# Gate and up products of a SwiGLU feed-forward network by seven block products in place of eight

## The chip, the cores and the metric

One core of a Trainium2 chip runs the kernel. TensorE (PE) multiplies, VectorE (DVE), ScalarE (ACT) and GpSimd (POOL) do the elementwise work, SyncE (SP) issues the loads of weights. The metric is the device time of one execution in microseconds (us).

## The reference, cut to what matters

One decoder layer works on 1056 token rows of width 1024: 1024 of a prompt and 32 samples. A mixer (a matrix memory beside sparse attention) ends in an output projection, a residual sum and a layer normalisation. The feed-forward network (FFN) follows, with 2816 hidden columns:

```python
D_FF = -(-8 * D_MODEL // (3 * 256)) * 256        # 2816
ALPHA = (2 * DEPTH) ** 0.25
h = jax.nn.silu(x @ w_gate) * (x @ w_up)          # 1056 x 2816
y = layer_norm(ALPHA * x + h @ w_down, g2, b2)
```

Everything is float32. The change concerns `x @ w_gate` and `x @ w_up` alone.

## The kernel before, in words

A float32 operand is kept as two parts: a high part (rounded to the type that TensorE takes) and a low part (the rest). `PARTS` lists the three products high-high, high-low and low-high that stand for one product. ScalarE makes high parts by a copy, GpSimd (for `x` of the mixer also VectorE) makes low parts by a subtraction.

**First normalisation.** `x` comes out of the output projection in nine row tiles (eight of 128, one of 32 that holds the samples), each in two column halves. VectorE adds the product bank to the residual (L1673, ALPHA x plus the product), takes statistics, adds epsilon, ScalarE takes the root (`std`), VectorE inverts it and centres the row (L1696). TensorE transposes the tile, ScalarE puts it with gain and bias into `y_acc` (`put_turned`), VectorE makes the high part `xs` (`high_of`), GpSimd the low part (L1725) and scales `y_acc` by ALPHA (L1731), so that `y_acc` can take the down product's sums.

**FFN.** The hidden columns are taken in 11 groups of 256 (`GROUPS`), each as two units `u` of 128. A unit needs 128 columns of the gate and of the up weights; SP loads the two pieces, 512 KB each, into one raw buffer `graw` (`sp_ffn.gate`), ScalarE copies the 2048 columns to the high part (`high`, L1865), GpSimd makes the low part (`low`, L1947). Two such pairs of split weights stand in turns. TensorE takes the 1056 rows in three chunks of 352 columns; per chunk, gate and up are each a sum over eight k tiles of three products: 2 x 2 x 3 x 8 x 3 = 288 matmuls of 352 columns per group (L1830), and 3168 in all. ScalarE takes silu of the gate bank (L1873), VectorE multiplies it by the up bank (L1911), copies the high part (`tensor_copy`, L1915) and subtracts to the low part (L1919).

The down product of group g-1 stands between the two units of group g: 144 matmuls of 352 columns (L1808), whose 24 banks VectorE adds to `y_acc` (L1816). The loops run over the groups on every engine; the last two groups' down products are done in the second normalisation (`pe_y`), ahead of the output.

The order on each engine is the order of the code; semaphores hold an instruction back. On SP the load of a unit waits for the low part of the one before (`g_lo`), since there is one raw buffer. GpSimd's order in the loop is `low(g, 1)`, `low(g + 1, 0)`, `low_down(g)`; VectorE's is the hidden columns of unit 0, the adds of the down product, the hidden columns of unit 1.

## Time and profile before

| what | value |
|---|---|
| three runs | 1586.88, 1587.2 and 1593.45 us; median 1587.2 |
| span of the profiled execution | 1586.6 us (no separate time is given for it) |
| TensorE busy | 1546.0 us, 97% |
| VectorE, ScalarE, GpSimd busy | 49%, 28%, 26% |
| gate and up matmuls (L1830) | 3168, 32% of the span in the chain that ended last |
| down matmuls in the loop (L1808) | 1296, 13% |

The span is the time from the first to the last recorded instruction. The chain that ended last follows the work back from the end, at each step to what released it. In a timeline row, the bracket behind an instruction is the idle time ahead of it on its engine and the instruction that ended it. Matmuls overlap in the pipeline, so a matmul's duration in a row is longer than the pitch at which they follow each other; a pitch is the time of a whole chain step divided by its matmuls.

### The profile page before, as it was taken

Reading aid. Unit: us, or ns where it says so; the run is one execution under the profiler, and the core shown is the slowest. Engines: PE = TensorE matmul, PEld = TensorE weight load, DVE = VectorE, ACT = ScalarE, POOL = GpSimd, SP = SyncE. Lnnn points to the kernel's source line nnn. Section 1 sums busy time; section 2 is a strip of 40 time slices with the busy share of each in tenths; the row PEclk is TensorE's granted clock in tenths of the full one; section 3 lists DMA queues with packets and bytes.
Section 4 is the critical chain, followed back from the end, with each engine's and each line's share of the span. In section 5 each row is a group of like instructions: output and inputs, shape, how many; then the busy total and the mean of one; then the engine's idle time right before and its main releaser. Section 6 shows DMA issues by size and latency. Waiting matters only on the chain.

```text
span 1586.6 us, 26851 instructions
## 1 busy us (share of the span) xinstructions
PE 1546.0 (97%) x10593; PEld 1435.2 (90%) x10593; DVE 772.3 (49%) x1664; ACT 451.5 (28%) x929; POOL 412.3 (26%) x405
## 2 busy tenths in 40 slices
PE   7999999999999998899999999999999999999998
PEld 7986799999996666687899999999999999999986
DVE  2008599999965664563653323324132332313146
ACT  4336423222145564361352120221112012111100
POOL 3620256321110002453683221221122122112200
PEclk9999999999999999999999999999999999999999
DMA  5210231222317004543202101101111111111011
GB/s 187 72 44 19 65 101 41 71 83 85 104 46 258 28 27 130 161 128 123 67 27 80 53 27 54 54 30 51 54 54 27 54 54 36 45 54 54 1 61 76
DMA packets 117236, 110.52 MB, mean 70 GB/s; under 512 B 16218, under 2 KB 102366, under 8 KB 117122
## 3 DMA queue, kind: packets, MB, share of 16 engines
q1 hardware_dynamic: 116482, 106.80, 21.6%
q0 software_dynamic: 640, 2.10, 0.4%
q8 instruction: 84, 1.38, 0.3%
q14 instruction: 30, 0.25, 0.0%
HBM read 88.82 MB, written 19.95 MB: 69 GB/s over the span
## 4 chain that ended last, share of the span: by engine, by line
PE 58%; POOL 0%; DVE 0%; issue 0%; DVEq 0%
PE bank L1830 32%; PE bank L1808 13%; PE bank L1599 6%; PE bank L1993 3%; PE bank L1988 0%; PE bank L1748 0%; PE bank L1167 0%; PE bank L1595 0%; PE bank L1170 0%; POOL c_and_n_sample L1317 0%; PE bank L1133 0%; PE bank L1153 0%; PE bank L1182 0%; PE bank L1103 0%; POOL mv_by_sample L1313 0%
## 5 line engine op out<-in xcount | busy, mean ns | idle before, releaser
L1830 PE MATMUL bank<-x_split,gate_up_split 128*128 128x352 f32 x3168 | 509.9, 322 | 0.0
L1830 PEld LDWEIGHTS bank<-x_split,gate_up_split 128*128 128x128 f32 x3168 | 507.3, 188 | 0.1
L2284 PE MATMUL bank<-w_split,xT_split 128*128 128x256 f32 (+1 forms) x1950 | 247.7, 284 | 3.7 <-POOL w_split L2517 2.0
L2284 PEld LDWEIGHTS bank<-w_split,xT_split 128*128 128x128 f32 (+1 forms) x1950 | 234.3, 187 | 8.2 <-issue 3.7
L1911 DVE TENSOR_TENSOR hidden<-silu,bank 128x352 f32<-128x352 f32 x66 | 34.4, 521 | 408.5 <-ACT silu L1873 408.5
L1808 PE MATMUL bank<-hidden_split,weight_split 128*128 128x352 f32 x1296 | 209.2, 322 | 0.0
L1808 PEld LDWEIGHTS bank<-hidden_split,weight_split 128*128 128x128 f32 x1296 | 208.0, 188 | 0.0
L1947 POOL TENSOR_TENSOR gate_up_split<-gate_up,gate_up_split 128x2048 fp32r<-128x2048 f32 x22 | 104.1, 4734 | 370.7 <-ACT gate_up_split L1865 370.7
L2622 DVE TENSOR_SCALAR_CACHE_REDUCE chosen<-scores,level 128x384 uint8<-128x384 f32 (+2 forms) x198 | 174.3, 943 | 1.2
L1816 DVE TENSOR_TENSOR y_acc<-y_acc,bank 128x352 f32<-128x352 f32 x216 | 112.5, 521 | 84.6 <-PE bank L1808 83.4
L2341 PE MATMUL bank<-xT_split,w_split 128*128 128x352 f32 x864 | 138.4, 322 | 0.0
L2341 PEld LDWEIGHTS bank<-xT_split,w_split 128*128 128x128 f32 x864 | 138.2, 188 | 0.0
L1873 ACT ACTIVATE silu<-bank 128x352 f32<-128x352 f32 x66 | 30.6, 464 | 364.3 <-PE bank L1830 364.2
L2517 POOL TENSOR_TENSOR w_split<-w_unit,w_split 128x2048 fp32r<-128x2048 f32 (+1 forms) x16 | 72.2, 4514 | 147.7 <-ACT w_split L2362 147.7
L1951 POOL TENSOR_TENSOR weight_split<-down_weight,weight_split 128x2048 fp32r<-128x2048 f32 x10 | 46.1, 4606 | 159.5 <-ACT weight_split L1879 159.5
L1599 PE MATMUL bank<-out_weight_split,x_split 128*128 128x512 f32 (+1 forms) x342 | 81.6, 396 | 0.0
L1599 PEld LDWEIGHTS bank<-out_weight_split,x_split 128*128 128x128 f32 (+1 forms) x342 | 63.4, 186 | 15.5
L2410 ACT ACTIVATE stage<-bank 128x256 f32<-128x256 f32 x80 | 30.7, 384 | 161.2 <-PE bank L2284 150.7
L1879 ACT ACTIVATE weight_split<-down_weight 128x2048 fp32r<-128x2048 f32 x10 | 19.1, 1915 | 186.6 <-PE bank L1808 186.6
L545 ACT ACTIVATE attention_weights<-attention_weights,row_minima 128x1024 f32<-128x1024 f32 (+7 forms) x64 | 49.1, 768 | 46.9 <-DVE row_minima L476 46.8
L476 DVE CUSTOM_DVE_ANT_0 attention_weights<-bank,scores 128x512 f32<-128x512 f32 (+1 forms) x48 | 30.1, 666 | 50.2 <-PE bank L387 50.2
L1865 ACT ACTIVATE gate_up_split<-gate_up 128x2048 fp32r<-128x2048 f32 x22 | 42.1, 1913 | 22.5 <-DMA gate_up<-in_w_up_dram 22.4
(310 smaller groups left out, 1703.3 us busy)
## 6 DMA issues: line engine op xcount, KB each, us to landing
w_unit<-in_w_in_dram SPq DMA_DIRECT2D x15, 1024.0 KB, 5.7
gate_up<-in_w_gate_dram SPq DMA_DIRECT2D x22, 512.0 KB, 4.0
gate_up<-in_w_up_dram SPq DMA_DIRECT2D x22, 512.0 KB, 5.2
down_weight<-in_w_down_dram SPq DMA_DIRECT2D x11, 1024.0 KB, 4.9
scratch_dram<-feature_stage SPq DMA_DIRECT2D x36, 176.0 KB, 1.8
scores<-in_x_prompt_dram SPq DMA_DIRECT2D x8, 512.0 KB, 3.9
out_dram<-stage SPq DMA_DIRECT2D x32, 128.0 KB, 1.7
out_weight<-in_w_out_dram SPq DMA_DIRECT2D x16, 256.0 KB, 6.2
```

Source lines behind the costliest of these rows:

```text
L545: act.activation(x, x, ACT.Exp, bias=lows[:, n % 4, e, chunks[n] - 1:chunks[n]], scale=-1.0, accum_out=rowsum[:, o % 2, 2 * p + e:2 * p + ...
L1599: mm = pe.matmul(product_bank(m)[0:rows(i), :], mix(i, a)[:, k, :], wo[h][:, k, b, :], start=(k == 0 and (a, b) == PARTS[0]), stop=(i < LA ...
L1808: mm = pe.matmul(PS[6 + n % 2][:, 0:cols.stop - cols.start], wds[:, a, k, d * P:(d + 1) * P], hs[:, 2 * s + k, b, cols], start=(k == 0 and ...
L1816: dve.tensor_tensor(y, y, PS[6 + n % 2][:, 0:cols.stop - cols.start], ALU.add).then_inc(d_added, 1)
L1830: mm = pe.matmul(PS[2 * c + w][:, 0:CH], gs[u][:, a, w, k, :], xs[:, b, k, c * CH:(c + 1) * CH], start=(k == 0 and (a, b) == PARTS[0]), st ...
L1947: pool.tensor_tensor(gs[u][:, 1], graw, gs[u][:, 0].bitcast(F32), ALU.subtract).then_inc(g_lo, 1)
L1951: pool.tensor_tensor(w[:, 1], wdraw, w[:, 0].bitcast(F32), ALU.subtract).then_inc(wd_lo, 1)
L1993: mm = pe.matmul(bank, hs[:, 2 * s + k, a, tile_cols(i)], w[:, b, k, 512 * half:512 * half + 512], start=False, stop=(s == 0 and k == 1 an ...
L2284: mm = pe.matmul(out, tokens, w[:, b, k, :], start=((k, a, b) == terms[0]), stop=((k, a, b) == terms[-1]))
L2341: mm = pe.matmul(bank[:, 0:CH], wsplit[n_unit % 2][:, a, k, (m % 2) * P:(m % 2 + 1) * P], xs1[:, b, k, c * CH:(c + 1) * CH], start=(k == 0 ...
L2517: pool.tensor_tensor(lo, wraw[n >= 4][:, k], hi.bitcast(F32), ALU.subtract).then_inc(w_lo, 1)
L2622: dve.tensor_scalar(chosen[i], score[i], level_f[:, n:n + 1], 0.0, op, ALU.add, accum_out=count[:, n:n + 1]).then_inc(topk_step, 1)
```

## The change

The 1056 rows of `x` and the 1024 inner columns are halved, and so are the 256 columns of a group. A matrix (the gate or up weights of one group; 22 in all) then has four blocks A11, A21, A12, A22 of 512 x 128, and its product is formed from seven block products (`multiply`, j = 0 to 6) in place of eight, after Strassen and Winograd. Each block product is two chunks of 272 and 256 columns, four k tiles and `PARTS`: 24 matmuls (L2049), 168 per matrix, 3696 in all. The order of a matrix's factors is A11, A12, three weight sums with A12 changed among them, A22 (`part_source`), against `XPARTS`. Banks 0 and 1, 2 and 3, 4 and 5 each gather two or three block products; banks 6 and 7 stay with the down product.

- **Weights.** SP loads a matrix's two halves of 512 KB into one raw buffer (`load`, L1972); half 1 of the next matrix waits for the low part of j = 6 of this one. A ring of four slots holds the split blocks; ScalarE copies 128x512 to the high part (`high_part`, L1962), GpSimd subtracts to the low part (`low_part`, L1966). GpSimd forms four weight sums per matrix (`weight_sums` and `last_weight_sum`, L2174 to L2184) ahead of the low part of j = 2, in place in the raw buffer. The down weights pass through the same ring as four parts.
- **Sums of x.** T1 to T4 are formed by VectorE in the first normalisation (`halves_of`), split by ScalarE and GpSimd. The row tiles come in the order 0, 1, 2, 3, samples, 4, 5, 6, 7.
- **Results.** ScalarE puts the first product into SBUF (`put_p1`, L2104). VectorE adds bank 2 and 3 to it twice (`products_16`, L2190, and `products_165`, L2196) and makes the second to fourth quarter of the result from it and a bank (`result`, L2215: r1, r2, r3). For an up matrix it also multiplies by silu (`hide`, L2229) and splits (`split_hidden`, L2237 and L2241). TensorE's next writes to a bank wait for the result that reads it: j = 0 of the next matrix waits for r2, j = 3 for r3.
- The scaling by ALPHA moves into the first down product's add. The reloads of ScalarE's function tables fall from the loop.

The core of the diff (what stands beside it is the order of the tiles and the stores of samples):

```diff
+HT = T // 2
+CO, CW = (0, 272), (272, HT - 272)
+raw = put("gate_up", R0, KD * 2 * P).rearrange("p (k n) -> p k n", k=KD)
+A11, A21, A12, A22 = raw[:, 0:4, 0:P], raw[:, 0:4, P:2 * P], raw[:, 4:8, 0:P], raw[:, 4:8, P:2 * P]
+RING_W = 4
...
+stages = []
+for g in range(GROUPS):
+    stages += [("gate", g)] + ([("down", g - 1)] if 0 < g < GROUPS - 1 else []) + [("up", g)]
+parts = [(kind, g, j) for kind, g in stages for j in range(4 if kind == "down" else 7)]
...
+XPARTS = (B11, B21, T2, T3, T1, B22, T4)
+BANK_OF = (0, 0, 2, 4, 2, 0, 4)
+BEGINS = (0, 2, 3, 5)
...
+def part_free(eng, e):
...
+def part_source(e):
+    kind, g, j = parts[e]
+    if kind == "down":
+        return slots_raw[:, e % RING_W, 1, :].rearrange("p (k n) -> p k n", k=2)
+    return (A11, A12, A11, A21, s1_sum, A12, A22)[j]
...
+def high_part(act, e):
+    kind, g, j = parts[e]
+    n = stage_no_of(kind, g)
+    part_free(act, e)
+    if kind == "down":
+        act.wait_ge(wd_in[j % 2], 16 * (2 * g + j // 2 + 1))
+    elif j in (0, 1, 6):
+        act.wait_ge(raw_in[j > 0], 16 * (n + 1))
+    else:
+        act.wait_ge(summed, summed_no(n, j))
+    act.activation(slot(e, 0), part_source(e), ACT.Copy).then_inc(slot_hi, 1)
+def low_part(pool, e):
+    pool.wait_ge(slot_hi, e + 1)
+    pool.tensor_tensor(slot(e, 1), part_source(e), slot(e, 0).bitcast(F32), ALU.subtract).then_inc(slot_lo, 1)
...
+    def load(n, half):
+        kind, g = ("gate", "up")[n % 2], n // 2
+        if n == 0:
+            sp.wait_ge(norms["first"]["nT"], 2 * 5)
+        elif half == 0:
+            before = part_no[("gate", "up")[(n - 1) % 2], (n - 1) // 2, 0]
+            sp.wait_ge(summed, summed_no(n - 1, 5))
+            sp.wait_ge(slot_lo, before + 4)
+        else:
+            before = part_no[("gate", "up")[(n - 1) % 2], (n - 1) // 2, 0]
+            sp.wait_ge(slot_lo, before + 7)
+        k = slice(4 * half, 4 * half + 4)
+        sp.dma_start(raw[:, k, :], weights[n % 2][:, k, 2 * P * g:2 * P * g + 2 * P]).then_inc(raw_in[half], 16)
...
+    def multiply(n, j, c):
+        e = part_no[("gate", "up")[n % 2], n // 2, j]
+        pe.wait_ge(slot_lo, e + 1)
+        if n == 0:
+            if j < 2:
+                pe.wait_ge(x1_lo, (6, 10)[c])
+            elif j < 6:
+                pe.wait_ge(x1_lo, (lows_before(6), lows_before(8))[c] + j - 1)
+            else:
+                pe.wait_ge(x1_lo, lows_before(TILES) + c + 1)
+            if j in (2, 3):
+                pe.wait_ge(added, 2 * TILES)
+        elif j in (0, 2, 3):
+            pe.wait_ge(combined, combined_no(n - 1, {0: "r2", 2: "p165", 3: "r3"}[j], c))
+        if j == 1:
+            pe.wait_ge(p1_put, 2 * n + c + 1)
+        if j == 4:
+            pe.wait_ge(combined, combined_no(n, "p16", c))
+        if j == 5:
+            if n % 2:
+                pe.wait_ge(h_made, 16 * (n // 2) + c + 1)
+            else:
+                pe.wait_ge(silu_done, silu_no(n // 2, 0, c))
+        if j == 6:
+            pe.wait_ge(combined, combined_no(n, "r1", c))
+        for k in range(4):
+            for a, b in PARTS:
+                mm = pe.matmul(PS[BANK_OF[j] + c][:, 0:CW[c]], slot(e, a)[:, k, :],
+                               XPARTS[j][:, b, k, CO[c]:CO[c] + CW[c]],
+                               start=(j in BEGINS and k == 0 and (a, b) == PARTS[0]),
+                               stop=(k == 3 and (a, b) == PARTS[-1]), skip_group_check=True)
+        mm.then_inc(product, 1)
...
+def weight_sums(eng, n):
+    e = part_no[("gate", "up")[n % 2], n // 2, 0]
+    for half in range(2):
+        eng.wait_ge(raw_in[half], 16 * (n + 1))
+    if n:
+        eng.wait_ge(slot_lo, part_no[("gate", "up")[(n - 1) % 2], (n - 1) // 2, 4] + 1)
+    s1 = s1_sum if n else s1_first
+    eng.tensor_tensor(s1, A21, A22, ALU.add).then_inc(summed, 1)
+    eng.tensor_tensor(A21, A11, A21, ALU.subtract).then_inc(summed, 1)
+    eng.wait_ge(slot_lo, e + 1)
+    eng.wait_ge(summed, summed_no(n, 3))
+    eng.tensor_tensor(A11, s1, A11, ALU.subtract).then_inc(summed, 1)
+def last_weight_sum(eng, n):
+    e = part_no[("gate", "up")[n % 2], n // 2, 0]
+    eng.wait_ge(slot_lo, e + 2)
+    eng.wait_ge(summed, summed_no(n, 2))
+    eng.tensor_tensor(A12, A12, A11, ALU.subtract).then_inc(summed, 1)
...
+def products_16(dve, n, c):
+    dve.wait_ge(product, product_no(n, 2, c))
+    dve.wait_ge(p1_put, 2 * n + c + 1)
+    dve.tensor_tensor(p16[:, c, 0:CW[c]], p1[:, c, 0:CW[c]], PS[2 + c][:, 0:CW[c]], ALU.add).then_inc(combined, 1)
+def products_165(dve, n, c):
+    dve.wait_ge(product, product_no(n, 4, c))
+    dve.wait_ge(combined, combined_no(n, "p16", c))
+    dve.tensor_tensor(p1[:, c, 0:CW[c]], p1[:, c, 0:CW[c]], PS[2 + c][:, 0:CW[c]], ALU.add).then_inc(combined, 1)
...
+    def matrix(kind, g):
+        n, e = stage_no_of(kind, g), part_no[kind, g, 0]
+        more(e)
+        put_p1(act, n, 0)
+        put_p1(act, n, 1)
+        for j in range(1, 7):
+            more(e + j)
+            if kind == "gate" and j != 2 and j != 3:
+                q = {1: 0, 4: 1, 5: 2, 6: 3}[j]
+                silu(act, g, q, 0)
+                silu(act, g, q, 1)
+            if n == 2 * GROUPS - 1 and j in (4, 6):
+                last_high((j - 4) // 2)
...
+    def matrix(kind, g):
+        n = stage_no_of(kind, g)
+        up = kind == "up"
+        if up:
+            hide(g, 0, 0)
+            hide(g, 0, 1)
+        products_16(dve, n, 0)
+        products_16(dve, n, 1)
+        if up:
+            split_hidden(g, 0)
+        for c in range(2):
+            products_165(dve, n, c)
+            result(dve, n, 1, c)
+        if up:
+            hide(g, 1, 0)
+            hide(g, 1, 1)
+            split_hidden(g, 1)
+        result(dve, n, 2, 0)
+        result(dve, n, 2, 1)
+        if up:
+            hide(g, 2, 0)
+            hide(g, 2, 1)
+            split_hidden(g, 2)
+        result(dve, n, 3, 0)
+        result(dve, n, 3, 1)
+        if up:
+            hide(g, 3, 0)
+            hide(g, 3, 1)
+            split_hidden(g, 3)
...
+    def halves_of(t):
+        i = SWEEP2[t]
+        c1, c = first_half(i), second_half(i)
+        dve.wait_ge(nm["nput"], 2 * t + 1)
+        if i < 4 or i == LAST:
+            dve.tensor_copy(B11[:, 0, :, c1], yh[:, 0:4, 0, c1]).then_inc(x1_hi, 1)
+        if i >= 4:
+            dve.tensor_tensor(T1_raw[:, :, c], yh[:, 0:4, 1, c], yh[:, 0:4, 0, c], ALU.subtract).then_inc(t_sum, 1)
+        dve.wait_ge(nm["nput"], 2 * t + 2)
+        if i < 4 or i == LAST:
+            dve.tensor_copy(B21[:, 0, :, c1], yh[:, 4:8, 0, c1]).then_inc(x1_hi, 1)
+        if i >= 4:
+            done = 4 * SUMMED.index(i)
+            dve.tensor_tensor(T3_raw[:, :, c], yh[:, 4:8, 1, c], yh[:, 0:4, 1, c], ALU.subtract).then_inc(t_sum, 1)
+            dve.wait_ge(t_sum, done + 1)
+            dve.tensor_tensor(T2_raw[:, :, c], yh[:, 4:8, 1, c], T1_raw[:, :, c], ALU.subtract).then_inc(t_sum, 1)
+            dve.tensor_copy(B22[:, 0, :, c], yh[:, 4:8, 1, c]).then_inc(x1_hi, 1)
+            dve.wait_ge(t_sum, done + 3)
+            dve.tensor_tensor(T4_raw[:, :, c], yh[:, 4:8, 0, c], T2_raw[:, :, c], ALU.subtract).then_inc(t_sum, 1)
...
+    for t in range(TILES - 3):
+        lows(t)
+    low_part(pool, 0)
+    low_part(pool, 1)
+    lows(TILES - 3)
+    low_part(pool, 2)
+    low_part(pool, 3)
+    low_part(pool, 4)
+    lows(TILES - 2)
+    low_part(pool, 5)
+    lows(TILES - 1)
```

The order of the instructions moves at three places. On GpSimd, in the loop over groups, the program before ran (`gate_up_split` are the two pairs of split weights, ISA rows are its semaphore operations):

```order
L1947 TENSOR_TENSOR gate_up_split_138<-gate_up,gate_up_split_138 128x2048
L1946 ISA
L1947 TENSOR_TENSOR gate_up_split_137<-gate_up,gate_up_split_137 128x2048
L1951 TENSOR_TENSOR weight_split<-down_weight,weight_split 128x2048
L1956 REGISTER_ALU
L1956 COMPARE_AND_BRANCH
```

and the changed one, from one matrix's first weight sum to the split of the down weights:

```order
L2174 TENSOR_TENSOR weight_sum<-gate_up 128x512
L2175 TENSOR_TENSOR gate_up<-gate_up 128x4x128
L2178 TENSOR_TENSOR gate_up<-weight_sum,gate_up 128x4x128
L2184 TENSOR_TENSOR gate_up<-gate_up 128x4x128
L1966 TENSOR_TENSOR weight_split<-gate_up,weight_split 128x512 x2
L1966 TENSOR_TENSOR weight_split<-weight_sum,weight_split 128x512
L1966 TENSOR_TENSOR weight_split<-gate_up,weight_split 128x512 x2
L1966 TENSOR_TENSOR weight_split<-down_weight,weight_split 128x512 x4
```

Two subtractions of 2048 columns per group have become 14 of 512 columns and eight sums; the four sums stand one behind the other, ahead of the third low part of their matrix.

On VectorE, from the fifth block product of an up matrix on (`product` is p1, `hidden_sum` the result's quarter, `bank` is in PSUM, the rest in SBUF):

```order
L2196 TENSOR_TENSOR product_154<-product_154,bank 128x272
L2215 TENSOR_TENSOR hidden_sum<-product_154,bank 128x272
L2196 TENSOR_TENSOR product_154<-product_154,bank 128x256
L2215 TENSOR_TENSOR hidden_sum<-product_154,bank 128x256
L2229 TENSOR_TENSOR hidden<-hidden,hidden_sum 128x272
L2229 TENSOR_TENSOR hidden<-hidden,hidden_sum 128x256
L2237 CAST hidden_split<-hidden 128x272
L2237 CAST hidden_split<-hidden 128x256
L2241 TENSOR_TENSOR hidden_split<-hidden,hidden_split 128x272
L2241 TENSOR_TENSOR hidden_split<-hidden,hidden_split 128x256
L2215 TENSOR_TENSOR hidden_sum<-product_154,bank 128x272
L2215 TENSOR_TENSOR hidden_sum<-product_154,bank 128x256
```

Ahead of the two L2215 rows that end it (r2, for which TensorE's next matrix waits) stand six instructions on operands in SBUF (two products, two copies, two subtractions); before, the three instructions of a chunk's hidden columns read its bank at once, and nothing of the next chunk stood behind them in the same bank.

On GpSimd, at the start of the first gate matrix (L1830 and L1833 are low parts of T2, T3, T1 and B22 of a row tile, L1966 are weights):

```order
L1966 TENSOR_TENSOR weight_split<-gate_up,weight_split 128x512 x2
L1830 TENSOR_TENSOR x_sums<-x_sums_raw,x_sums 128x4x128 x2
L1830 TENSOR_TENSOR x_split<-x_split_raw,x_split 128x4x128
L1833 TENSOR_TENSOR x_split<-y_acc,x_split 128x4x128
L1966 TENSOR_TENSOR weight_split<-gate_up,weight_split 128x512 x2
L1966 TENSOR_TENSOR weight_split<-weight_sum,weight_split 128x512
L1830 TENSOR_TENSOR x_sums<-x_sums_raw,x_sums 128x4x128 x2
L1830 TENSOR_TENSOR x_split<-x_split_raw,x_split 128x4x128
L1833 TENSOR_TENSOR x_split<-y_acc,x_split 128x4x128
L1966 TENSOR_TENSOR weight_split<-gate_up,weight_split 128x512
```

The low parts of the first weights stand between those of `x`: parts 2 to 4 behind the low parts of row tile 6's quarter, part 5 behind the next tile's.

## Rows read from the trace of the kernel before

**Rows 1.** The page, part 1: busy us (share of the span) xinstructions.
```profile
PE 1546.0 (97%) x10593; PEld 1435.2 (90%) x10593; DVE 772.3 (49%) x1664; ACT 451.5 (28%) x929; POOL 412.3 (26%) x405
```

**Rows 2.** The chain that ended last, in time: start us, us, engine, output, line.
```profile
793.88 5.59 PE bank L1599 x24
...
876.34 23.09 PE bank L1808 x144
899.43 46.10 PE bank L1830 x288
...
1452.87 69.16 PE bank L1830 x432
```

**Rows 3.** TensorE timeline, two stretches: start us, us, line, shapes, count.
```profile
187.26 8.40 PE L2284 MATMUL bank<-w_split,xT_split 128*128 128x256 f32 x69 [1.18 <-POOL w_split L2517]
...
320.13 22.89 PE L2284 MATMUL bank<-w_split,xT_split 128*128 128x256 f32 x192
342.85 0.28 PE L2284 MATMUL bank<-w_split,sample_x_split 128*64 128x256 f32 x1
```

**Rows 4.** Groups by line and form: busy us, mean ns of one; VectorE within 870 to 1450 us.
```profile
L1725 POOL TENSOR_TENSOR x_split<-y_acc,x_split 128x512 fp32r<-128x512 f32 x16 | 20.8, 1302 | 11.5 <-DVE x_split L1702 11.5
...
L2410 ACT ACTIVATE stage<-bank 128x256 f32<-128x256 f32 x80 | 30.7, 384 | 161.2 <-PE bank L2284 150.7 <-PE bank L2301 5.5 <-PE bank L2266 4.8
L1638 ACT ACTIVATE out_weight_split<-out_weight 128x512 fp32r<-128x512 f32 x16 | 8.8, 632 | 19.4 <-DMA out_weight<-in_w_out_dram 19.4
...
L1919 DVE TENSOR_TENSOR hidden_split<-hidden,hidden_split 128x352 fp32r<-128x352 f32 x50 | 26.2, 524 | 1.4
L1915 DVE CAST hidden_split<-hidden 128x352 fp32r<-128x352 f32 x50 | 17.1, 343 | 1.4
```

**Rows 5.** DMA issues: transfer, queue, count, KB each, median us to landing.
```profile
gate_up<-in_w_gate_dram SPq DMA_DIRECT2D x22, 512.0 KB, 4.0
gate_up<-in_w_up_dram SPq DMA_DIRECT2D x22, 512.0 KB, 5.2
```

**Rows 6.** VectorE and GpSimd timelines, single instructions near 707 and 1086 us.
```profile
705.43 0.69 DVE L1631 TENSOR_TENSOR x_split<-mixT,x_split 128x512 fp32r<-128x512 f32 x1 [0.24 <-ACT x_split L1621]
...
708.35 1.78 DVE L1631 TENSOR_TENSOR x_split<-mixT,x_split 128x512 fp32r<-128x512 f32 x1
...
707.84 1.74 POOL L1631 TENSOR_TENSOR x_split<-mixT,x_split 128x512 fp32r<-128x512 f32 x1
...
1086.35 4.94 POOL L1947 TENSOR_TENSOR gate_up_split<-gate_up,gate_up_split 128x2048 fp32r<-128x2048 f32 x1 [17.10 <-ACT gate_up_split L1865]
...
1086.80 0.52 DVE L1816 TENSOR_TENSOR y_acc<-y_acc,bank 128x352 f32<-128x352 f32 x1
```

**Rows 7.** TensorE and ScalarE timelines near 1045 us: start us, us, idle before, what ended it.
```profile
1037.62 12.55 PE L1830 MATMUL bank<-x_split,gate_up_split 128*128 128x352 f32 x77
...
1045.64 0.46 ACT L1873 ACTIVATE silu<-bank 128x352 f32<-128x352 f32 x1 [5.91 <-PE bank L1830]
```

**Rows 8.** VectorE timeline of the first normalisation, row tile 6.
```profile
793.11 0.69 DVE L1673 SCALAR_TENSOR_TENSOR x_tm<-x_tm,bank 128x512 f32<-128x512 f32 x1 [1.45 <-PE bank L1599]
...
797.22 0.91 DVE L1696 TENSOR_SCALAR x_tm<-x_tm,moments,rstd 128x1024 f32<-128x1024 f32 x1
```

**Rows 9.** TensorE timeline: three pauses, the idle time before in brackets.
```profile
612.58 1.20 PE L714 MATMUL bank<-sample_scores,square 32*128 32x288 f32 x4 [1.40 <-DVE mixT L519]
...
650.15 0.27 PE L1080 MATMUL bank<-mixT,mkT 128*32 128x32 f32 x8 [2.25 <-DVE mq_scaled L1342]
...
668.67 0.50 PE L1066 MATMUL bank<-g_split,head_rows_split 128*128 128x512 f32 x1 [1.94 <-DVE kT L1335]
```

**Rows 10.** Stretches around them: us, TensorE busy (x), granted clock, DMA share, GB/s.
```profile
613.00:618.00 5.00, 5.00 (x28) 0.66 0.72 209
650.00:656.00 6.00, 5.85 (x113) 0.72 0.74 295
666.00:672.00 6.00, 4.06 (x34) 1.00 0.18 59
```

## The forecast

> **What bounds the kernel now.** I read the page first: TensorE is busy 97% of the span, the next engine 49% [rows 1]. The page's busy share is not yet the limit, so I read the chain of waits next. From 876 us on it has TensorE steps alone: 144 down matmuls, 288 gate and up matmuls, and so on to 1522 us, where the last run of 432 (the second unit of group 9 and both of group 10) ends [rows 2]. In this stretch nothing but matmuls counts: what leaves TensorE there leaves the span, and every wait put onto TensorE is added to it. The other engines have slack on average, but a share of busy time says nothing of the order in which they work; so the question is whether the new chain TensorE, VectorE, GpSimd, ScalarE keeps TensorE fed at each handover.
>
> **What leaves TensorE.** 288 matmuls of 352 columns take 46.10 us [rows 2], a pitch of 160.1 ns; a matrix is half of this, 23.05 us. For 256 columns, 192 matmuls took 342.85 - 320.13 = 22.72 us, 118.3 ns each [rows 3]. No 272 occurs; the straight line through both points gives 0.435 ns a column and 125.3 ns. A block product is 12 x 125.3 + 12 x 118.3 ns = 2.92 us, a matrix of seven 20.46 us. Over 22 matrices that takes off 22 x (23.05 - 20.46) = **56.9 us**. Bounds: at a cost in proportion to columns (116.4 and 123.7 ns) it is 63.4; at the slowest dense stretch of 256, 8.76 us for 72 or 121.7 ns [rows 3], and 7 ns more for 272, it is 44.4. I take the line, since both its points are long runs without a break.
>
> **What an instruction costs on the others.** A low part or weight sum of 128x512 on GpSimd: 1.30 us; a high part on ScalarE 0.63; `put_p1` about the 0.38 of a 256-column copy from PSUM [rows 4]. On VectorE a subtraction of 352 columns 0.52, a copy 0.34 [rows 4], an add from a bank 0.52 [rows 6]; at 272 and 256 I scale to 0.40 and 0.27. A load of 512 KB lands 4.0 us after its issue, 5.2 as the second of a pair [rows 5]. From TensorE's last matmul to the next engine's start: 48 matmuls from 1037.62 on end 0.2 us before the silu at 1045.64 [rows 7].
>
> **Two engines that block each other.** A VectorE operation with two SBUF operands took 0.69 us alone and 1.78 us while GpSimd ran; GpSimd's took 1.74 there [rows 6] in place of 1.30 [rows 4]. Each seems to go when the other has ended, a pair in about 1.7 us. VectorE's add from a bank took 0.52 us in the midst of a GpSimd subtraction [rows 6]: not blocked. The Trainium skill, page "SBUF — State Buffer", section "SBUF: two separate sides", gives it as a rule: the pair of ports that VectorE and GpSimd share is locked for a whole instruction, by VectorE when it has two SBUF inputs. By that rule the trace agrees, 1.78 against 0.69; without it the handover below would cost next to nothing.
>
> **Handover from an up matrix to the next gate matrix.** Time 0 is the up matrix's first matmul, block product j ends at 2.92 (j + 1). GpSimd splits j = 6 when the slot of j = 2 is free: 8.77, plus ScalarE's copy, plus 1.30: 10.95. Only then may SP load half 1 of the next weights into the raw buffer; it lands at 15.1, ScalarE has copied it by 15.8, and GpSimd starts there on one low part, four sums and two low parts, 7 x 1.30 us without a gap. VectorE, after p165 and r1 of the fifth block product (ended 14.6), comes at 15.7 to `hide`, `split_hidden`: six instructions on SBUF alone, 2.2 us by themselves. By turns with GpSimd they take six pairs: 15.7 + about 8.2 to 9.7 = 23.9 to 25.4 before r2 can begin, and r2 of the first chunk has to be done by 20.46 for TensorE not to wait. The pause is 3.5 to 4.9 us; bounds are 1.9, if the load lands 1 us later (VectorE is then further along), and 5.5, if GpSimd always goes first. I take 4.0; there are ten of these handovers: **+40 us**. Were there no turns, r2 would start at 17.9 to 18.9, in time. From gate to up, VectorE has only bank operands in front of r2, so nothing: `put_p1` has 0.36 us to spare. Behind the pause nothing is late next: r3 has three block products of time.
>
> **The first gate matrix.** Time 0 is here the end of the out-projection's last tile but one; the last ends at 6.5, its 5.59 [rows 2] and some 0.9 for a tile's transpositions. GpSimd's queue holds four low parts of `x` per tile (5.2 us alone, 6.8 by turns with VectorE) between those of weights. The first weights' low part is done at 13.45: a wait of 7.0. Slot 2 stands behind the low parts of the next tile: 6.4. Slot 5 behind those of the one after: 6.0. VectorE forms the first weight sums itself, behind a first low part, and so adds the last tile at 15.65 only; from that add to the end of the centring takes 5.0 us (793.11 to 798.13) [rows 8], and `put_p1` stands behind its root: 2.25. The second chunk of p16 stands behind T4, which waits for all of GpSimd's low parts: 3.75. The seventh block's copy stands behind silus: 3.1. The first up matrix's half 1 is loaded only after the low part of j = 6, then come low part, three sums and a copy: 6.7. Together **+35 us**. Without the turns each row of GpSimd shortens and it is 29; if a load lands late and both wait in full, 45.
>
> **The end.** At the last group, one pause of 0.5 ahead of the last up matrix, and 3.6 ahead of the second normalisation, where VectorE is blocked by the four low parts of the last down weights: **+4 us**. The eight sums and eighteen low parts per group (33.8 us of GpSimd beside some 64 us of TensorE) and the loads (as many bytes as before, on SP's queue, where a load of down weights can stand behind the wait of a half 1) are hidden but for the places named; if this cover were gone, each low part would cost 1.3 us. The scaling by ALPHA and ScalarE's table loads were off the path: nothing.
>
> **The clock.** After a pause of 1.40 us on TensorE the granted clock was 0.66 over 5 us, after one of 2.25 it was 0.72 over 6 us, after one of 1.94 it stayed 1.00 [rows 9, 10]: mixtures of full (2.4 GHz) and half (1.2 GHz). Such a drop costs 5 x 0.34 or 6 x 0.28 = 1.7 us. A pause of 4 us is longer than all three, so I take a drop after each of the ten: **+17 us**; the bounds from the rows are 0 and 17. In the first matrix the other engines set the pace, so a slower TensorE costs little more. The Trainium skill, page "TensorE: Matmul & The Clock Gate", Part 1, says that the half rate is the default and that activity releases it. By that rule each of the ten pauses is likely to bring it back; the third pause of 1.94 us, with 1.00 behind it, shows that not every one does.
>
> **Sum.** 1586.6 - 56.9 + 35 + 40 + 4 + 17 = 1625.7, say **1626 us**. The profiled execution's span of 1586.6 stands 0.6 us below the median of the three runs, too little to shift it. About 0.5% (8 us) is what a measurement of this kernel can tell from no change.
>
> **The rivals.**
> - **The engines do not collide** (faster). The six VectorE instructions slip between GpSimd's, or the load lands so that the sums come after r2; handovers cost under 1 us and the clock stays. 1586.6 - 56.9 + 29 + 5 = 1564. For it: the VectorE work by itself would be done over 1 us before TensorE needs it, and GpSimd is idle three quarters of the time now. Against it: the two starts of 15.7 and 15.8 lie upon each other, and the slow pair of rows 6. It decides if r2 starts before about 20. Chance 0.20.
> - **The gain is eaten** (no change). The turns are there, but loads land a microsecond later and the pause is the 1.9 of the lower bound, too short for the clock: 1586.6 - 56.9 + 32 + 19 + 4 = 1585. For it: 5.2 us of the up loads in rows 5. Against it: one load at a time is in flight here, as in the 4.0. Chance 0.14.
> - **The smaller matmuls do not pay** (slower). If a narrower matmul is held by its weight load, the pitch would not fall with the columns. The point of equality is 3168 x 160.1 / 3696 = 137.2 ns. At 150 ns the matmuls would take 554 against 507 us; a matrix would take 25.2 us, so that r2 would be in time at the handovers, and the sum is 1586.6 + 47 + 35 + 4 = 1673. Rows 3 show 118.3 and at worst 121.7 ns. Chance 0.03.
> - The forecast, with pauses of 3 to 5 us at ten handovers: chance 0.63, by itself between 1600 (no clock drops and 29 at the start) and 1651 (5.5 a pause, 45 at the start).
>
> **How the numbers follow.** The forecast's own end of 1651 is moved to 1655 for the matmuls' upper bound; below, the range goes down to 1562 and takes in the no-change case and about half of the first rival. Outside are some 0.09 below, 0.03 of the third rival and some 0.05 of the forecast's own tails: under 0.2. Faster by over 0.5% is the first rival, 0.20; within 0.5% the second, 0.14; slower the other two, 0.66.
>
> **What would show it.** In the changed kernel: TensorE's L2049 idle for about 4 us at the first matmul of ten gate matrices, ended by VectorE's L2215; VectorE's L2229, L2237 and L2241 at 1.3 us or more ahead of those; pauses of 6 to 7 us ended by GpSimd's L1966 in the first matrix; a granted clock below 1.00 behind the pauses; L2049 at about 450 us in all. It is wrong if r2 is done ahead of the next matrix, if the pauses stand elsewhere (a load, `put_p1`), if the clock stays at 1.00, or if the pitch of 272 is far from 125 ns.

## The result: 1.2% slower, half of what was forecast

| | time |
|---|---|
| the kernel before | median 1587.18 us of 4 runs |
| the changed kernel | median 1607.67 us of 4 runs (1607.26 to 1609.70) |
| ratio | 1.0116, 95% interval 1.0103 to 1.0129 |
| forecast | 1626 us, range 1562 to 1655, slower at 0.66 |

The direction and the mechanism were right, the time lies inside the range, and the size is off by half: +20.5 us measured, +39 forecast. The profiled execution took 1607.92 us, with a span of 1606.1 us, 19.5 more than that of before. All sums below are of spans.

From the page of the changed kernel: part 1 (busy time, share, instructions) and the costliest group of part 5 (busy and mean ns, then the idle time ahead of it and what ended most of it).

```profile
PE 1514.2 (94%) x11119; PEld 1399.6 (87%) x11119; DVE 954.7 (59%) x1974; ACT 507.6 (32%) x1153; POOL 619.2 (39%) x643
...
L2049 PE MATMUL bank<-x_split,weight_split 128*128 128x272 f32 (+1 forms) x2112 | 282.0, 295 | 40.8 <-DVE hidden_sum L2215 21.5
```

TensorE is busy 1514.2 us where it was 1546.0 [rows 1]: the matmuls did become cheaper. What the page says at once is the last number of the second row: 21.5 us of TensorE's idle time ended by `hidden_sum`, L2215, which is VectorE's r2.

**Where the matmuls' gain came from.** The chain that ended last, in time (start us, us, engine, output, line), from the second up matrix on, and the first gate matrices behind it:

```profile
906.20 23.11 PE bank L2085 x144
929.31 14.60 PE bank L2049 x120
...
952.53 20.67 PE bank L2049 x168
...
1019.59 22.16 PE bank L2049 x168
```

120 matmuls take 14.60 us, 121.7 ns each; the forecast's line through the points for 352 and 256 columns [rows 2, 3] gave 121.8. A matrix of 168 is 20.44 us, and 22 x (23.05 - 20.44) = 57.4 us leave TensorE (forecast 56.9). The second row of 168 took 22.16 us, and that is the clock, below.

**Where it went.** TensorE's timeline, the rows with a pause of over 0.5 us ahead of them (the bracket: idle us and what ended it). Those from 1087.06 to 1361.08 that are left out repeat the one of 1019.59, 2.77 to 2.86 us.

```profile
811.10 7.93 PE L2049 MATMUL bank<-x_split,weight_split 128*128 128x272 f32 x48 [5.63 <-POOL weight_split L1966]
...
826.07 5.81 PE L2049 MATMUL bank<-x_sums,weight_split 128*128 128x272 f32 x24 [6.16 <-POOL weight_split L1966]
...
836.24 1.78 PE L2049 MATMUL bank<-x_split,weight_split 128*128 128x272 f32 x12 [2.87 <-POOL weight_split L1966]
...
844.81 4.59 PE L2049 MATMUL bank<-x_split,weight_split 128*128 128x256 f32 x24 [3.51 <-DVE products L2190]
852.22 4.71 PE L2049 MATMUL bank<-x_sums,weight_split 128*128 128x272 f32 x24 [2.82 <-POOL weight_split L1966]
...
864.32 5.39 PE L2049 MATMUL bank<-x_split,weight_split 128*128 128x272 f32 x24 [4.48 <-ACT product L2104]
888.46 3.16 PE L2049 MATMUL bank<-x_split,weight_split 128*128 128x272 f32 x24 [1.24 <-ACT product L2104]
952.53 6.08 PE L2049 MATMUL bank<-x_split,weight_split 128*128 128x272 f32 x48 [2.80 <-DVE hidden_sum L2215]
1019.59 7.58 PE L2049 MATMUL bank<-x_split,weight_split 128*128 128x272 f32 x48 [2.90 <-DVE hidden_sum L2215]
...
1087.06 7.61 PE L2049 MATMUL bank<-x_split,weight_split 128*128 128x272 f32 x48 [1.80 <-DVE hidden_sum L2215]
...
1361.08 7.49 PE L2049 MATMUL bank<-x_split,weight_split 128*128 128x272 f32 x48 [2.77 <-DVE hidden_sum L2215]
1430.42 3.16 PE L2049 MATMUL bank<-x_split,weight_split 128*128 128x272 f32 x24 [0.83 <-ACT product L2104]
1494.46 7.38 PE L2049 MATMUL bank<-x_split,weight_split 128*128 128x272 f32 x48 [2.77 <-DVE hidden_sum L2215]
1520.14 3.16 PE L2049 MATMUL bank<-x_split,weight_split 128*128 128x272 f32 x24 [0.80 <-ACT product L2104]
1541.77 2.90 PE L2337 MATMUL bank<-weight_split_last,hidden_split_last 128*128 128x512 f32 x6 [2.07 <-DVE hidden_split_last L2241]
```

The ledger is read from the same row marks in both traces:

| stretch | before | after | difference without the matmuls' gain | forecast |
|---|---|---|---|---|
| up to the end of the first three matrices | ends 876.34 | ends 906.20 | 29.9 + 3 x 2.61 = 37.7 | 35, and 5.7 for one handover and its clock |
| the loop: 19 matrices and 9 down products | 645.7 us (to 1522.03) | 631.5 us (to 1537.7) | 19 x 2.61 - 14.2 = 35.4 | 36 + 15.3 (nine handovers and their clock) + 0.5 |
| the second normalisation | 58.2 us | 62.0 us | 3.8 | 3.6 |

With the matmuls' 57.4 off, that is 19.5. The first and the last stretch came about as forecast (3 us less and none); the loop came 16.4 us cheaper. Of its 35.4 us, 22.3 are the pauses at nine handovers, 0.8 the one at 1520.14, some 10.3 a slower clock; the 2 us that are left are not placed. The down products did not change (23.11 us for 144, [rows 2] 23.09).

The first stretch has another make-up than the forecast's. Its six pauses up to 864.32 are 25.5 us. Five of the rows behind them are longer than rows of as many matmuls further on (7.93 us against 6.08 for 48; 5.81, 4.59, 4.71 and 5.39 against 3.16 for 24), together some 9.7 us, while the granted clock was 0.83 from 812 to 864 us.

**One handover, instruction by instruction.** VectorE from the first `hide` on, then GpSimd, at the end of the up matrix whose first matmul began at 996.27 us (start us, us, form; "x2" is two instructions on end):

```profile
1011.76 2.98 DVE L2229 TENSOR_TENSOR hidden<-hidden,hidden_sum 128x272 f32<-128x272 f32 x2
1014.67 1.59 DVE L2237 CAST hidden_split<-hidden 128x272 fp32r<-128x272 f32 x2
1016.18 2.92 DVE L2241 TENSOR_TENSOR hidden_split<-hidden,hidden_split 128x272 fp32r<-128x272 f32 x2
1019.02 0.75 DVE L2215 TENSOR_TENSOR hidden_sum<-product,bank 128x272 f32<-128x272 f32 x2
...
1011.74 1.28 POOL L1966 TENSOR_TENSOR weight_split<-gate_up,weight_split 128x512 fp32r<-128x512 f32 x1 [1.76 <-ACT weight_split L1962]
1012.98 1.48 POOL L2174 TENSOR_TENSOR weight_sum<-gate_up 128x512 f32<-128x512 f32 x1
1014.42 1.48 POOL L2175 TENSOR_TENSOR gate_up<-gate_up 128x512 f32<-128x512 f32 x1
1016.04 1.34 POOL L2178 TENSOR_TENSOR gate_up<-weight_sum,gate_up 128x512 f32<-128x512 f32 x1
```

The two engines start their lists 0.02 us apart, as the forecast had it (15.5 us after the matrix's start; 15.7 and 15.8 forecast). Two `hide` instructions, alone 0.4 us each, take 2.98; two subtractions 2.92. GpSimd's sums take 1.48 in place of 1.29. The six take 7.26 us and r2 starts at 1019.02, 22.8 us after the start where 23.9 to 25.4 were forecast; TensorE, done at 1016.7, waits 2.90 us. At 1087.06 both lists begin at 1080.33, one `hide` slips through (1.87 us for the two), and the pause is 1.80 us.

At the end of group 8 the same instructions:

```profile
1421.75 0.77 DVE L2229 TENSOR_TENSOR hidden<-hidden,hidden_sum 128x272 f32<-128x272 f32 x2
1422.44 0.50 DVE L2237 CAST hidden_split<-hidden 128x272 fp32r<-128x272 f32 x2
1422.85 1.86 DVE L2241 TENSOR_TENSOR hidden_split<-hidden,hidden_split 128x272 fp32r<-128x272 f32 x2
1424.63 0.75 DVE L2215 TENSOR_TENSOR hidden_sum<-product,bank 128x272 f32<-128x272 f32 x2
...
1422.83 1.60 POOL L1966 TENSOR_TENSOR weight_split<-gate_up,weight_split 128x512 fp32r<-128x512 f32 x1 [2.87 <-ACT weight_split L1962]
```

Here the weights landed 1.1 us later after the matrix's start, GpSimd began at 1422.83, and VectorE was by then through both `hide` and both copies (0.77 and 0.50 us). Five turns became one, r2 began at 1424.63, and no pause of r2 stands in the list above at 1430.42, only 0.83 us that ScalarE's `put_p1` ends. The first gate matrix's handover (888.46) is of that kind too.

**The clock.** Two stretches behind pauses of nearly the same length (us, TensorE busy, granted clock, DMA share, GB/s):

```profile
952.50:960.10 7.60, 7.57 (x62) 1.00 0.24 69
1019.50:1027.20 7.70, 7.61 (x50) 0.78 0.25 68
```

After 2.80 us of idle the clock stayed at 1.00; after 2.90 us it was 0.78, a mixture of the two levels, and 48 matmuls took 7.58 in place of 6.08 us: 1.50 us for a drop. One came behind seven of the eight long pauses, one of them (1087.06) of 1.80 us. The seven rows of 48 matmuls are 1.30 to 1.53 us longer than 6.08, some 10.3 us in all, where the forecast had ten drops of 1.7.

### The profile page after: what moved, and what is told of

It is laid out like the page before. It is cut to its first block, busy times and chain, and to the rows that moved or that the text cites. A ratio compares the mean times of both kernels' runs of the same rounds, so it can differ in the third digit from the quotient of the medians.

```text
span 1606.1 us, 28886 instructions
## 1 busy us (share of the span) xinstructions
PE 1514.2 (94%) x11119; PEld 1399.6 (87%) x11119; DVE 954.7 (59%) x1974; ACT 507.6 (32%) x1153; POOL 619.2 (39%) x643
## 4 chain that ended last, share of the span: by engine, by line
PE 48%; DVE 5%; issue 3%; POOL 3%; ACT 0%; DVEq 0%; POOLq 0%; ACTq 0%
PE bank L2049 23%; PE bank L2085 13%; PE bank L1666 5%; PE bank L2337 3%; DVE hidden L2229 1%; DVE hidden_split L2237 1%; DVE hidden_split L2241 1%; POOL weight_split L1966 1%; PE bank L2328 0%; POOL x_sums L1830 0%; PE bank L1167 0%; PE bank L1170 0%; PE bank L1858 0%; POOL c_and_n_sample L1317 0%; PE bank L1133 0%
## 5 line engine op out<-in xcount | busy, mean ns | idle before, releaser
L2049 PE MATMUL bank<-x_split,weight_split 128*128 128x272 f32 (+1 forms) x2112 | 282.0, 295 | 40.8 <-DVE hidden_sum L2215 21.5
L2049 PEld LDWEIGHTS bank<-x_split,weight_split 128*128 128x128 f32 x2112 | 276.4, 199 | 43.9 <-issue 34.6
L1966 POOL TENSOR_TENSOR weight_split<-gate_up,weight_split 128x512 fp32r<-128x512 f32 x132 | 175.1, 1331 | 201.4 <-ACT weight_split L1962 201.3
L2049 PE MATMUL bank<-x_sums,weight_split 128*128 128x272 f32 (+1 forms) x1584 | 204.2, 288 | 9.2 <-POOL weight_split L1966 9.0
L2049 PEld LDWEIGHTS bank<-x_sums,weight_split 128*128 128x128 f32 x1584 | 199.6, 191 | 9.8 <-POOL weight_split L1966 9.4
L1962 ACT ACTIVATE weight_split<-gate_up 128x512 fp32r<-128x512 f32 x132 | 82.0, 630 | 355.7 <-POOL gate_up L2178 113.0
L1666 PE MATMUL bank<-out_weight_split,x_split 128*128 128x512 f32 x336 | 80.3, 396 | 0.0
L1966 POOL TENSOR_TENSOR weight_split<-down_weight,weight_split 128x512 fp32r<-128x512 f32 x36 | 46.5, 1293 | 83.4 <-ACT weight_split L1962 83.4
L1666 PEld LDWEIGHTS bank<-out_weight_split,x_split 128*128 128x128 f32 x336 | 62.5, 188 | 14.5
L2241 DVE TENSOR_TENSOR hidden_split<-hidden,hidden_split 128x272 fp32r<-128x272 f32 x80 | 64.4, 844 | 0.0
```

Of the source, the lines that this page charges most:

```text
L1666: mm = pe.matmul(product_bank(m), mix(i, a, k // 4)[:, k % 4, :], wo[h][:, k, b, :], start=(k == 0 and (a, b) == PARTS[0]), stop=(k == KD ...
L1962: act.activation(slot(e, 0), part_source(e), ACT.Copy).then_inc(slot_hi, 1)
L1966: pool.tensor_tensor(slot(e, 1), part_source(e), slot(e, 0).bitcast(F32), ALU.subtract).then_inc(slot_lo, 1)
L2049: mm = pe.matmul(PS[BANK_OF[j] + c][:, 0:CW[c]], slot(e, a)[:, k, :], XPARTS[j][:, b, k, CO[c]:CO[c] + CW[c]], start=(j in BEGINS and k == ...
L2241: dve.tensor_tensor(dst[:, m, 1, cols], sg[:, m, cols], dst[:, m, 0, cols].bitcast(F32), ALU.subtract)\
```

## The experiments

Ratios are to the kernel before on the same chip, whose median was 1589.8 us for the first four, 1589.5 for the next four and 1588.9 for the last three.

### 1. r2 ahead of the SBUF-only instructions

```diff
+                result(dve, n, 2, 0)
+                result(dve, n, 2, 1)
                 if up:
                     hide(g, 1, 0)
                     hide(g, 1, 1)
                     split_hidden(g, 1)
-                result(dve, n, 2, 0)
-                result(dve, n, 2, 1)
```

> Edit: in the up matrices VectorE makes r2 (two adds from a bank) ahead of the six SBUF-only instructions of the second quarter (hide, split) in place of behind them; nothing else moves. Theory T (turns): r2 is late because those six take turns with GpSimd's sums, about 1.5 us a pair. Then the pauses of about 2.8 us on TensorE that r2 ends (eight of ten handovers, 21.5 us) go, and the slower clock behind seven of them (1.5 us each, 10.6 us) with them; what is next, the copy of the first product on ScalarE, costs 0.8 us as at the one handover of group 8 that had no such pause. 1607.7 - 21.5 - 10.6 + 8 x 0.8 = about 1582, 1573 to 1586. Rival B (load and weights): TensorE would wait at that place anyway, for the next matrix's weights; the pause changes its name to L1966 or L2104 at 2 to 3 us: 1600 to 1608.

Measured: 1584.9 us, ratio 0.9968 (0.9954 to 0.9982), 1.5% off the changed kernel's ratio. The pauses of r2 are gone, and no clock drop is left behind the handovers. What is late next is VectorE again, with the turns still taken but behind r2: r3 and p16 hold TensorE by about 0.56 and 0.41 us at each handover; at the first and at group 8 the put holds it by 1.16 and 0.90 us as well. Theory B falls: TensorE waited for the place of r2 in VectorE's list. Whether turns or the mere number of instructions made that place late is for the next two experiments.

```profile
1092.28 3.16 PE L2049 MATMUL bank<-x_sums,weight_split 128*128 128x272 f32 x24 [0.56 <-DVE hidden_sum L2215]
...
1095.84 6.07 PE L2049 MATMUL bank<-x_split,weight_split 128*128 128x272 f32 x48 [0.41 <-DVE products L2190]
```

### 2. GpSimd's sums wait for r2

```diff
+            if n and n % 2 == 0:
+                eng.wait_ge(combined, combined_no(n - 1, "r2", 1))
             for half in range(2):
                 eng.wait_ge(raw_in[half], 16 * (n + 1))
```

> Edit: GpSimd's four weight sums of a gate matrix wait until r2 of the up matrix before is done; VectorE's order is that of the change. Theory T: the six VectorE instructions run alone (about 2 us), r2 is done by 18.7 us after the up matrix's start, and GpSimd's chain begins some 6 us later, ending just ahead of TensorE's need of the third part; pauses of r2 gone: 1578 to 1590. Rival A (VectorE's order alone, six instructions too many ahead of r2 whatever GpSimd does): no gain, 1605 to 1610. Rival B (weights are late anyway): the third part is late, 2 to 3 us at each of ten handovers in its place: 1605 to 1620.

Measured: 1612.2 us, ratio 1.0144 (1.0128 to 1.0161). The time lies in rival B's range, but by another wait than B's. VectorE, ScalarE and TensorE, at the end of an up matrix:

```profile
1080.58 1.76 DVE L2231 TENSOR_TENSOR hidden<-hidden,hidden_sum 128x272 f32<-128x272 f32 x2
1082.27 0.49 DVE L2239 CAST hidden_split<-hidden 128x272 fp32r<-128x272 f32 x2
1082.68 0.76 DVE L2243 TENSOR_TENSOR hidden_split<-hidden,hidden_split 128x272 fp32r<-128x272 f32 x2
1083.37 0.76 DVE L2217 TENSOR_TENSOR hidden_sum<-product,bank 128x272 f32<-128x272 f32 x2
...
1090.02 1.15 ACT L1962 ACTIVATE weight_split<-gate_up 128x512 fp32r<-128x512 f32 x2 [9.67 <-POOL gate_up L2180]
1091.07 0.65 ACT L2104 ACTIVATE product<-bank 128x272 f32<-128x272 f32 x2
...
1091.59 4.68 PE L2049 MATMUL bank<-x_split,weight_split 128*128 128x272 f32 x24 [3.17 <-ACT product L2104]
```

VectorE's six instructions take 2.8 us from 1080.58 on, only the first delayed, and both chunks of r2 are done by 1084.13, 1.4 us ahead of TensorE's next matrix (the up matrix began at 1065.09 and takes 20.44 us): the order of VectorE alone was not too long (rival A falls). But the sums now begin 2.5 us later, ScalarE's copy of a summed block (L1962, 1090.02) waits for them, and `put_p1` (L2104) stands behind that copy in ScalarE's list. TensorE waits 3.17 us for the put here, 3.2 to 3.3 at three other handovers and 1.8 to 1.9 at five: a wait took the place of the one removed, on another engine.

### 3. Four short SBUF-only instructions more

```diff
                     split_hidden(g, 1)
+                    for i in range(4):
+                        dve.wait_ge(x1_hi, highs_before(TILES) + 4 * g)
+                        dve.tensor_tensor(spare[:, i], sg[:, 0, 0:48], sg[:, 0, 48:96], ALU.add).then_inc(x1_hi, 1)
                 result(dve, n, 2, 0)
```

> Edit: four more VectorE instructions on two SBUF operands, 48 columns each (about 0.15 us alone), ahead of r2 in every up matrix; they write to unused space. Theory T: each that meets a running GpSimd operation costs a turn of 1.5 us, however short it is; GpSimd's chain has about 2.6 us left there, so about two turns: +3 us at each of the eight handovers that pause, 1 to 3 at the other two, so +26 to +32, 1633 to 1640. Rival A (sheer length of VectorE's list, no turns): 4 x 0.15 us at eight to ten handovers, +5 to +6: 1613.

Measured: 1641.5 us, ratio 1.0328 (1.0311 to 1.0345). The pauses are 5.4 to 5.6 us where they were 2.8, and group 8's handover has one of 2.25. The four instructions (`spare`) took 2.72 us beside GpSimd's last two low parts, the two turns that were expected, and r2 came that much later. The time is 1.5 us above the expected range; the clock stays low for longer behind these pauses (48 matmuls in 8.42 us, not 7.58). Rival A's 1613 is far off.

```profile
1024.30 2.72 DVE L2281 TENSOR_TENSOR spare<-hidden 128x48 f32<-128x48 f32 x4
1026.94 0.76 DVE L2216 TENSOR_TENSOR hidden_sum<-product,bank 128x272 f32<-128x272 f32 x2
...
1024.05 2.66 POOL L1967 TENSOR_TENSOR weight_split<-gate_up,weight_split 128x512 fp32r<-128x512 f32 x2
...
1027.51 8.42 PE L2050 MATMUL bank<-x_split,weight_split 128*128 128x272 f32 x48 [5.41 <-DVE hidden_sum L2216]
```

### 4. The first weight sums behind the last tile

```diff
-                    if t == LAST - 1:
-                        weight_sums(dve, 0)
+            weight_sums(dve, 0)
             dve.tensor_copy(s1_sum, s1_first).then_inc(summed, 1)
```

> Edit: in the first gate matrix VectorE's three weight sums stand behind the last row tile's normalisation in place of ahead of it. Theory S: they hold up the last tile's statistics and through them ScalarE, which stands at its root from 806.6 to 815.1 us with the high parts of x's sums and of part 2 behind it; 5 us less there shortens the pause of 6.2 us ahead of part 2: -4 to -7, 1601 to 1604. Rival G (GpSimd's low parts set the pace of this stretch): the pauses move, the end of the third matrix stays within 1.5 us: 1606 to 1609.

Measured: 1605.5 us, ratio 1.0095 (1.0078 to 1.0112). Against the changed kernel's 1.0116 that is between both expectations and within the intervals: the pause ahead of part 2 shrank from 6.16 to 4.29 us, but a following one grew from 2.87 to 3.45. Not decided here; the eleventh run takes it up.

### 5. ScalarE's put ahead of its copy

```diff
-                more(e)
                 put_p1(act, n, 0)
                 put_p1(act, n, 1)
+                more(e)
```

> Edit: at the start of every matrix ScalarE puts the first product into SBUF (L2104) ahead of the high part of the matrix's fourth weights (L1962), not behind it. Theory P: that copy waits for a weight sum, and the put behind it holds TensorE by 0.8 to 1.2 us where r2 does not (first gate matrix to second, group 8 to 9, the last up matrix) and by 4.5 us in the first up matrix; these go, the pauses of r2 stay: -4 to -7, 1601 to 1604. Rival: the later high parts make the low parts late by as much: 1606 to 1609.

Measured: 1609.5 us, ratio 1.0124 (1.0107 to 1.0141), no difference from the changed kernel. The four pauses shrank by 0.4 to 0.5 us each (0.83 to 0.31 at group 8), some 2 us in all, not the 4 to 7 expected: an earlier copy in ScalarE's list, that of the third block, waits for a sum as well (at group 8 it begins at 1432.34, behind 5.80 us of idle that GpSimd's L2178 ends, and the put follows at 1432.88).

### 6. Both: the sums' wait and the put ahead

The edits of the second and the fifth experiment together.

> Edit: both the wait of GpSimd's sums for r2 (as in the second experiment) and ScalarE's put ahead of its copy (as in the fifth). Theory T with P: the second experiment freed VectorE (its six instructions took 2.9 us in place of 7.3) and only put a new wait in the place of the old, ScalarE's put behind a copy that waits for the late sums; with the put ahead, the handover costs 0 to 0.5 us: 1573 to 1584. Rival B (the weights of the third part are late whatever the order): pauses ended by L1966 of 1.5 to 3 us in their place: 1595 to 1612.

Measured: 1598.7 us, ratio 1.0060 (1.0040 to 1.0080). The time lies in rival B's range, but again without B's wait: all pauses are ended by `put_p1`, 2.64 to 2.72 us at four handovers, 1.3 to 1.4 at four and 0.72 at two: the copy of the third block, one place earlier in the list, still waits for the late sums. So neither expectation holds in full; nothing was short of weights (no pause is ended by L1966 in the loop).

### 7. One instruction over both chunks

```diff
-                    hide(g, 1, 0)
-                    hide(g, 1, 1)
-                    split_hidden(g, 1)
+                    hide_both(g, 1)
+                    split_both(g, 1)
```

The same for the other quarters; `hide_both` and `split_both` do over 528 columns what stood there over 272 and 256.

> Edit: hide and split of an up matrix's second to fourth quarter, and the split of the first, are one instruction over both chunks (528 columns) in place of two (272 and 256); order and columns as in the change. Theory T (the number of turns counts, 1.5 us each, not the columns): three turns in place of five or six ahead of r2, 2 to 2.5 us earlier, so that the pauses of 2.8 us shrink to 0.5 to 1; with the clock kept or not 1583 to 1594. Rival C (the columns count: the two engines share the path by bandwidth): the same columns, the same time: 1605 to 1609.

Measured: 1581.1 us, ratio 0.9951 (0.9933 to 0.9968): with the order and the columns of the change, and half as many SBUF-only instructions, it is faster than before. VectorE and TensorE at a handover:

```profile
1074.11 1.48 DVE L2237 TENSOR_TENSOR hidden<-hidden,hidden_sum 128x528 f32<-128x528 f32 x1
1075.69 1.33 DVE L2244 CAST hidden_split<-hidden 128x528 fp32r<-128x528 f32 x1
1077.13 1.61 DVE L2246 TENSOR_TENSOR hidden_split<-hidden,hidden_split 128x528 fp32r<-128x528 f32 x1
1078.66 0.76 DVE L2215 TENSOR_TENSOR hidden_sum<-product,bank 128x272 f32<-128x272 f32 x2
...
1079.23 6.08 PE L2049 MATMUL bank<-x_split,weight_split 128*128 128x272 f32 x48 [0.41 <-DVE hidden_sum L2215]
```

Three instructions take 4.6 us where six took 7.3, r2 starts 2.5 us earlier against TensorE, the pause is 0.41 us and the clock stays. That decides between turns and columns: three turns are cheaper than five, for the same data. Group 8's handover has 1.30 us by the put. The time is 2 us under the expected range.

### 8. Four of the edits together

The first, fourth, fifth and seventh edit, and r3 ahead of the third quarter's `hide`.

> Edit: r2 first (first experiment), and r3 ahead of the third quarter's hide; first weight sums behind the last tile (fourth); put ahead of copy (fifth); merged hide and split (seventh). By T and P: the first experiment's time, less the 0.56 and 0.41 us of VectorE's r3 and p16 that are left at each of ten handovers, less 5 for the put and 2 for the first sums: 1565 to 1572, under the kernel before. If something else holds each handover by a microsecond: 1576 to 1584.

Measured: 1573.0 us, ratio 0.9908 (0.9890 to 0.9927). Of the ten handovers five have no pause at all, three have one of 0.2 us by p16, and the first and that of group 8 have 0.71 and 0.83 by the put. The time lies 1 us above the expected range; the put was set at 5 us there, and its pauses had given some 2 in the fifth experiment.

### 9. The load 0.9 us later

```diff
                     sp.wait_ge(slot_lo, before + 7)
+                    if n % 2 == 0:
+                        sp.wait_ge(product, product_no(n - 1, 3, 1))
```

> Edit: SP issues half 1 of a gate matrix's weights when TensorE has ended the up matrix's fourth product (some 0.9 us later than the change does, which waits for a low part alone); the order on every other engine is the change's. In the change's trace the handover of group 8 had its weights 1.1 us later than the others and no pause by r2. Theory T (who comes first): VectorE gets its first instructions done before GpSimd's chain begins, r2 is in time at nearly all handovers, 0.8 us for ScalarE's put are left: 1580 to 1590. Rival (the lower bound of the forecast, a pause that shrinks by as much as the load is later): 1.9 us at each handover, with the slower clock: 1596 to 1602. Rival B (a later load makes weights late): 1608 or more.

Measured: 1581.5 us, ratio 0.9957 (0.9942 to 0.9972), from an edit that only makes a load wait. From the second on TensorE's handovers are of two kinds now, 0.72 us by r2 or 0.49 by `put_p1`, without a clock drop:

```profile
948.40 6.09 PE L2051 MATMUL bank<-x_split,weight_split 128*128 128x272 f32 x48 [0.72 <-DVE hidden_sum L2217]
1016.01 3.16 PE L2051 MATMUL bank<-x_split,weight_split 128*128 128x272 f32 x24 [0.49 <-ACT product L2106]
...
1007.68 0.77 DVE L2231 TENSOR_TENSOR hidden<-hidden,hidden_sum 128x272 f32<-128x272 f32 x2
...
1008.58 1.44 POOL L1966 TENSOR_TENSOR weight_split<-gate_up,weight_split 128x512 fp32r<-128x512 f32 x1 [2.68 <-ACT weight_split L1962]
```

The last two rows show who came first: VectorE's list begins 0.9 us ahead of GpSimd's chain, both `hide` take 0.77 us, and r2 begins 3.98 us after the list where it was 7.26.

The forecast's lower bound said 1.9 us for this case; it is 0.5 to 0.7. Whether the change is slower or faster than before hangs on which of the two engines begins first by under a microsecond.

### 10 and 11. The first matrix as well

On top of the eighth: ScalarE makes the seventh block's high part ahead of two silus, T4's low part needs no longer wait for GpSimd's whole list, and r3 keeps its place in the last group.

```diff
-            for c in range(2):
-                silu(act, 0, 1, c)
-                silu(act, 0, 2, c)
+            silu(act, 0, 1, 0)
+            silu(act, 0, 2, 0)
             high_part(act, 6)
             high_part(act, 7)
+            silu(act, 0, 1, 1)
+            silu(act, 0, 2, 1)
...
-                dve.wait_ge(x1_lo, lows_before(TILES))
```

> Edit: the eighth experiment's kernel, and at the start of the first gate matrix ScalarE makes the high parts of the seventh block and of the first up weights ahead of two silus, the low part of T4 counts on a semaphore of its own so that it need not wait for all of GpSimd's low parts, and in the last group r3 stands behind the third quarter's hide as in the change. Theory F (the order on ScalarE and VectorE holds the first stage: GpSimd stood idle 9 us ahead of the seventh block's low part): the pauses of 2.8 and 3.8 us go and that of 2.4 shrinks: -5 to -8 against the eighth, ratio to before 0.986 to 0.988, 1564 to 1568. Rival G (GpSimd's and VectorE's work on x sets the pace of the stage): within 2 us of the eighth, ratio 0.990 to 0.992.

> Edit: the tenth experiment's kernel with the first weight sums back ahead of the last row tile, as in the change. If those sums hold ScalarE (theory S of the fourth experiment) it is 2 to 5 us slower than the tenth; if the stage's pace is set elsewhere, within 1.5 us of it.

Measured: 1564.2 us, ratio 0.9848 (0.9833 to 0.9863), 5 runs, for the tenth; 1568.6 us, 0.9871 (0.9855 to 0.9886) for the eleventh, which has the first sums where the change put them. The tenth's first three matrices end at 896.41, the eighth's at 902.80, the changed kernel's at 906.20. So the order of the first stage was a part of the start-up cost; ScalarE's order and T4's wait were changed at once and are not told apart. Of theory F's pauses that of 2.8 us is gone and that of 2.4 is 0.83, but that of 3.8, the put in the first up matrix, did not go: it is 4.74.

The eleventh is 4 us slower by its median, with intervals that overlap. Its profiled execution (1567.9 us) does not put that into the first stage: from the last three matmuls of the output projection to the end of the third matrix it takes 91.9 us (805.65 to 897.60), and so does the tenth's (804.54 to 896.41). In the fourth run the same stretch took 99.2 us (806.77 to 905.92) where the changed kernel's took 101.7 (804.54 to 906.20). By these executions, one of each, the first sums cost some 2.5 us there and next to nothing once the rest of the stage is changed; what makes the eleventh's median longer stays open.

The tenth is the best version found, 1.5% under the kernel before. What is left in it are 20 us of pauses in the first matrices and 2 at the end; the loop has next to none (0.65 us at most). The pause that grew:

```profile
855.21 5.08 PE L2049 MATMUL bank<-x_split,weight_split 128*128 128x272 f32 x24 [4.74 <-ACT product L2104]
```

## Why the prediction was right and where it failed

- **The matmuls' gain** (56.9): right, 57.4. The straight line for 272 columns held. One of the signs named missed: the page has L2049 busy for 486.2 us (282.0 and 204.2 in its two groups), not about 450; the slower clock is some 20 us of that, and the rest was not looked into.
- **The blocking of VectorE by GpSimd**: right as a mechanism, which experiments 2, 3, 7 and 9 show each from another side. The rule of the Trainium skill (page "SBUF — State Buffer", "SBUF: two separate sides") says that the loser waits for a whole instruction; by that rule the trace agrees, about 1.5 us for a `hide` of 0.4.
- **"I take 4.0; there are ten of these handovers"**: this step failed, in size and in number. The pause was 2.77 to 2.90 us at seven handovers and 1.80 at one, and two had none by r2; 23.6 us with the waits for the put, not 40. The price of a turn was set at about 1.7 us, by one pair [rows 6]; here it is about 1.5 (2.98 us for two `hide` of 272 and 256 columns, 1.48 for one of 528 in the seventh experiment), and one of the two copies goes through unblocked. So the six took 7.3 us, not 8.2 to 9.7. The two without a pause by r2 are the ones where the load landed about 1 us later; the forecast's lower bound of 1.9 for that case scaled the pause down, where in truth VectorE's first instructions passed ahead of the chain and their turns fell away altogether.
- **The clock** (17): half right. Drops came behind seven pauses and cost about 1.5 us each, some 10.3 us. That not every pause brings one was said; that two handovers had no pause to bring one was the same error as above.
- **The first matrix** (35): 36.5 in all, taking the 1.24 us of its own handover out of 37.7, but made up otherwise. The six pauses are 25.5 us: 5.63 and 6.16 (7.0 and 6.4 forecast), slot 5 with 2.87 (6.0), p16 behind T4 with 3.51 (3.75), the seventh block with 2.82 (3.1), the first up matrix with 4.48 (6.7); the put behind the root (2.25) cost no pause. Some 9.7 us are TensorE's slower clock, a term that the forecast had set at "little more": that step failed, too. The sum is right by luck, since 10 us too much for the pauses stood against next to nothing for the clock.
- **The end** (4): right as a sum, 0.80 and 3.8. Of the 3.8, the pause is 2.07 where 3.6 were forecast; six matmuls behind it took 2.90 us, and 1.55 further on.
- **The rivals**: the first, "the engines do not collide", did not come about, and its 1564 was not reached by the change. Experiments 1, 7 and 9 show how near it was: the same products in another order, with merged instructions or with a later load take 1581 to 1585, although turns are still taken in each. The forecast named the place where it decides, that the two starts "lie upon each other", and gave the rival 0.20; that a load 0.9 us later takes most of the loss away was not seen.

## What to carry to other kernels

Count the SBUF-only VectorE instructions that stand between a TensorE result and the bank that TensorE wants back, and put the read of the bank ahead of them: their price beside a running GpSimd was a turn each here, not their columns, so merging them is worth more than shortening them. Where two engines' lists start within a microsecond of each other, price the handover for both orders and give both a real chance; a mean pause times the number of handovers is the wrong model. When a wait is added to keep two engines apart, look at once for what stands behind the newly late instruction on a third engine.

## What the hardware showed that was not expected

- A pair of instructions that take turns is shorter than the sum of both alone: about 1.5 us, where a `hide` of 0.4 and a sum of 1.29 make 1.7.
- The length of a pause alone does not tell whether the clock falls: 2.80 us without a drop at 952.53, 1.80 us with one at 1087.06. What else decides was not looked into.
- An edit that only delays a load (experiment 9) made the kernel some 25 us faster (ratio 0.9957 in place of 1.0116). Waits that look free are worth trying in both directions.
